# A decoder step's compressed branch: the prompt's chunks worked together with the first sample's, and one load of cache chunks moved forward

## The reference, cut to what matters

```python
def nsa_compress(kv, w_ck1, w_ck2, w_cv1, w_cv2, pe_k, pe_v):
    ...
    def mlp(x, pe, w1, w2):
        x = (x + pe[None, None, :, None, :]).transpose(0, 3, 1, 2, 4).reshape(B, NSA_KV_HEADS, n_cmp, CMP_BLK * HEAD_DIM)
        return jax.nn.silu(x @ w1) @ w2
    kc = mlp(blocks[:, :, :, 0], pe_k, w_ck1, w_ck2)
    vc = mlp(blocks[:, :, :, 1], pe_v, w_cv1, w_cv2)
```

## Time and profile before

| | us |
|---|---|
| median of 3 runs (range) | 1182.02 (1179.38 to 1186.98) |
| the profiled execution, its own time | 1191.54 |
| its span in the trace | 1189.7 |
| PE, DVE, ACT, POOL busy | 1084.4, 617.1, 392.6, 69.9 |
| the key stage in the trace, from the prompt's last projection column to the last sample's keys | 182.8 to 455.0 |

### The profile page before, as it was taken

The page is one execution under the profiler, slowest core; times in us unless marked ns, Lnnn a source line. Parts: engine busy times, 40 slices in busy tenths (PEclk is TensorE's granted clock), DMA queues, the critical chain, the costliest instruction groups (busy, mean ns, idle before and its releaser), DMA issues.

```text
span 1189.7 us, 23077 instructions
## 1 busy us (share of the span) xinstructions
PE 1084.4 (91%) x8348; PEld 953.0 (80%) x8348; DVE 617.1 (52%) x1042; ACT 392.6 (33%) x725; POOL 69.9 (6%) x83
## 2 busy tenths in 40 slices
PE   3996999998989998989999898999999999999993
PEld 2996999887878886555555557999999999999993
DVE  4431673586778787765444436445543335553332
ACT  4120212333333335556444435332231112221223
POOL 2000001221112100000000000110000000000002
PEclk9998997798999896988999978999999999999997
DMA  7529218799999963256666651323333333332321
GB/s 248 178 79 222 79 40 230 188 241 246 268 265 275 273 209 115 90 187 202 212 200 205 212 177 36 89 71 88 88 106 89 94 85 89 94 97 72 90 71 72
DMA packets 180131, 177.61 MB, mean 149 GB/s; under 512 B 13063, under 2 KB 140676, under 8 KB 177700
## 3 DMA queue, kind: packets, MB, share of 16 engines
q1 hardware_dynamic: 178610, 171.33, 50.7%
q10 hardware_dynamic: 1458, 5.43, 1.4%
HBM read 170.83 MB, written 10.06 MB: 152 GB/s over the span
## 4 chain that ended last, share of the span: by engine, by line
PE 64%; SPq 18%; issue 6%; DMA 4%; DVE 3%; ACT 3%; POOL 0%; POOLq 0%; DVEq 0%; ACTq 0%
PE bank L662 59%; SPq L576 4%; PE bank L666 4%; SPq L498 3%; SPq L540 2%; SPq L564 2%; SPq L543 2%; SPq L491 2%; DMA low_arena<-in_cache_nsa_slc_kv_dram 1%; DMA low_arena<-in_consts_dram 1%; DMA high_arena<-in_cache_sb_kv_dram 1%; DMA high_arena<-in_w_in_dram 1%; ACT low_arena L1550 1%; SPq L504 0%; SPq L582 0%
## 5 line engine op out<-in xcount | busy, mean ns | idle before, releaser
L662 PE MATMUL bank<-high_arena 128*128 128x254 f32 (+8 forms) x1864 | 239.6, 346 | 16.5 <-DMA high_arena<-in_cache_sb_kv_dram 6.6
L662 PEld LDWEIGHTS bank<-high_arena 128*128 128x128 f32 (+5 forms) x1864 | 185.2, 152 | 53.6 <-issue 10.1
L2114 DVE TENSOR_TENSOR w_low<-high_arena,w_high 128x1024 fp32r<-128x1024 f32 x72 | 90.1, 1252 | 84.1 <-ACT w_high L1487 74.2
L666 PE MATMUL bank<-low_arena 128*128 128x128 f32 (+3 forms) x658 | 108.0, 309 | 28.0 <-DMA page_ids<-in_page_table_dram 14.7
L666 PEld LDWEIGHTS bank<-low_arena 128*128 128x128 f32 (+3 forms) x658 | 87.4, 164 | 39.6 <-issue 27.2
L1487 ACT ACTIVATE w_high<-high_arena 128x1024 fp32r<-128x1024 f32 x72 | 76.3, 1060 | 114.8 <-PE bank L662 113.8
L662 PE MATMUL bank<-a_high,w_high 128*128 128x256 f32 (+1 forms) x512 | 104.3, 285 | 5.3 <-issue 2.9
L662 PE MATMUL bank<-h_high,w_high 128*128 128x256 f32 (+1 forms) x512 | 103.1, 283 | 1.8 <-DVE h_low L2141 1.8
L662 PE MATMUL bank<-a_low,w_high 128*128 128x256 f32 (+1 forms) x512 | 103.8, 284 | 0.0
L662 PE MATMUL bank<-a_high,w_low 128*128 128x256 f32 (+1 forms) x512 | 103.5, 283 | 0.0
L662 PE MATMUL bank<-h_low,w_high 128*128 128x256 f32 (+1 forms) x512 | 103.3, 283 | 0.0
(11 more groups left out here) (218 smaller groups left out, 1583.6 us busy)
## 6 DMA issues: line engine op xcount, KB each, us to landing
low_arena<-in_cache_sb_kv_dram SPq DMA_DIRECT2D x128, 256.0 KB, 4.9
high_arena<-in_cache_sb_kv_dram SPq DMA_DIRECT2D x128, 256.0 KB, 3.7
high_arena<-in_cache_nsa_cmp_kv_dram SPq DMA_DIRECT2D x128, 128.0 KB, 5.2
high_arena<-in_w_up_dram SPq DMA_DIRECT2D x32, 512.0 KB, 4.1
high_arena<-in_w_down_dram SPq DMA_DIRECT2D x32, 512.0 KB, 4.2
high_arena<-in_w_in_dram SPq DMA_DIRECT2D x10, 1136.0 KB, 5.6
low_arena<-in_cache_nsa_slc_kv_dram SPq DMA_DIRECT2D x128, 64.0 KB
high_arena<-in_cache_nsa_slc_kv_dram SPq DMA_DIRECT2D x128, 64.0 KB, 2.4
```

The source lines that it names most:

```text
L662: return T.matmul(out, lhsT=l, rhs=r, start=start, stop=stop, **k)
L666: return T.transpose(out, in_, ident[0:n, 0:n])
L2114: V.tensor_tensor(w_lo_r[u], w_raw[u], w_hi[u], ALU.subtract).then_inc(sem(f"w_lo{u}"), 1)
```

## The change

1. The prompt has no turn of its own. Its chunks are transposed first (`prompt_chunks_T`, 16 transposes), copied by ACT into `xTp`; in the turn of sample 0 each weight w1 is used three times in a row: for the prompt's 62 columns, for one column of `pe`, and for the sample's 254. All three results lie in the same PSUM bank. The 32 matmuls with one column that stood ahead of the prompt's turn are gone from there, and so are the waits of PE, ACT and DVE for `pebias`.
2. ACT does the sigmoid of sample 0 as six activations (prompt's and sample's), after a wait for `pebias`. DVE takes the bias out of PSUM (`bias(kv)`) after the quarter that ends each of the two sums, and so waits in the turn of sample 0 at four places: after pages 6, 8, 10 and 14.
3. The chunks of sample 1 (16 DMAs) are issued in the projection, behind the last w_in block, into a buffer moved to the end of memory; the prompt's chunks get a landing buffer of their own. `load_keys(0, 0)` loads no chunks.
4. SP waits for `snew` only ahead of the last ring buffer (page 7), not ahead of the stage.
5. POOL's waits are put in terms of transposes done in the same half. Loops start at 1, with turns 0 written out.

```diff
@@ -332,10 +333,14 @@
         w2 = [view(x_at + 4096 + i * DH, DH) for i in range(2)]
         pebias = view(x_at + 4224, 4)
         xT = [view(hT_at + i * 2048, KD, KVH, P) for i in range(2)]
-        nat_at[1] = r.take(4096)
+        nat_at[1] = TOTAL - 304 - 4096
+        nat_p = view(kc_at, CH // 2, 2, KVH, DH)
+        xTp = view(r_at, 2, KD, KVH, NCP + 1)
         nat = [[view(nat_at[u] + 2048 * half, CH // 2, 2, KVH, DH) for half in range(2)] for u in range(2)]
         hid = [view(r.take(256), KVH, P) for _ in range(4)]
         qb = view(r.take(2 * 512), 2, 512)
+        hidp = [view(r.take(KVH * NCP), KVH, NCP) for _ in range(4)]
+        assert r.at <= nat_at[1]
...
             load_columns(*COLUMNS[1])
+            for half in range(2):
+                load_chunks(page_ids(NPG + 8 * half), 1, half)
...
+                        if p == 7:
+                            sp.wait_ge(sem("snew"), 2)
...
-            sp.wait_ge(sem("snew"), 2)
-
-            with sp.Fori(0, 3) as i:
+
+            load_keys(0, 0, False)
+            load_keys(0, 1, True)
+            with sp.Fori(1, 3) as i:
...
-            for kv in range(2):
-                for m in range(16):
-                    ins = mm(bank[6][:, kv:kv + 1], w1[kv][:, m, :], vcol[:, 24 + 16 * kv + m:25 + 16 * kv + m],
-                             m == 0, m == 15)
-            ins.then_inc(sem("start_pe"), 1)
             for j in range(2):
                 pe.wait_ge(sem(f"qkT_ev{j}"), 7)
             pe.wait_ge(sem("qkT_ev0"), 8)
-            pe.wait_ge(*signal("pebias", 2))
...
+            def prompt_chunks_T(kv, qp):
+
+                pe.wait_ge(sem("perm"), kv + 1 + 1)
+                pe.wait_ge(sem(f"xT_ev{qp}"), kv + 1)
+                n = 2 * (NCP + 1)
+                for j in range(2):
+                    for hh in range(KVH):
+                        t = 2 * (2 * qp + j)
+                        ins = tr(bank[qp][:, (2 * j + hh) * P:(2 * j + hh) * P + n],
+                                 per(kv, hh, 0)[0:n, t:t + 2, :].rearrange("p t d -> p (t d)"))
+                ins.then_inc(sem(f"xT_mm{qp}"), 1)
...
+                    outp = bank[2 + kv][:, 256:256 + KVH * NCP].rearrange("p (h c) -> p h c", h=KVH)
                     for m in (2 * qp, 2 * qp + 1, 2 * qp + 4, 2 * qp + 5):
-                        mm(out, w1[kv][:, m, :], xT[kv][:, m, :, 0:nb], m == 0, False)
-                        ins = mm(out, w1[kv][:, 8 + m, :], xT[kv][:, m, :, 1:nb + 1], False, m == 7)
+                        for f in range(2):
+                            begin, end, w_ = m == 0 and f == 0, m == 7 and f == 1, w1[kv][:, 8 * f + m, :]
+                            if prompt:
+                                mm(outp, w_, xTp[:, kv, m, :, f:NCP + f], begin, end, skip_group_check=True)
+                                at = 24 + 16 * kv + 8 * f + m
+                                mm(bank[2 + kv][:, 320:321], w_, vcol[:, at:at + 1], False, end, skip_group_check=True)
+                            ins = mm(out, w_, xT[kv][:, m, :, f:NC + f], begin and not prompt, end, skip_group_check=prompt)
...
+            for kv in range(2):
+                for qp in range(2):
+                    prompt_chunks_T(kv, qp)
+            compress(0, key_work(0, 0), True)
+            compress(1, key_work(0, 1))
+            with pe.Fori(1, 4) as i:
                 for u in range(2):
-                    todo = [lambda: keys_T(i, u, 0)]
-                    for q in range(4):
-                        todo.append(lambda q=q: (key_scores(i, u, q), keys_T(i, u, q + 1)))
-                    todo.append(lambda: key_scores(i, u, 4))
-                    compress(i * 2 + u, 2, lambda: todo.pop(0)())
+                    compress(i * 2 + u, key_work(i, u))
...
-            act.wait_ge(*signal("pebias", 2))
...
+            def prompt_chunks_out(kv, qp):
+                act.wait_ge(sem(f"xT_mm{qp}"), kv + 1)
+                S.activation(xTp[:, kv].rearrange("p (f q) h c -> p f (q h) c", f=2)[:, :, 4 * qp:4 * qp + 4, :],
+                             bank[qp].rearrange("p (a c f) -> p f a c", a=4, f=2)[:, :, :, 0:NCP + 1],
+                             ACT.Copy).then_inc(sem(f"xT_ev{qp}"), 1)
+
+            def sample_keys(i, u, prompt=False):
...
+                    if prompt:
+                        act.wait_ge(*signal("pebias", kv + 1))
+                    both = [(hid[kv][:, :, 0:NC], 0, NC)] + ([(hidp[kv], 256, NCP)] if prompt else [])
+                    for e, at, n in both:
+                        ins = S.activation(e, bank[2 + kv][:, at:at + KVH * n].rearrange("p (h c) -> p h c", h=KVH),
+                                           ACT.Exp, bias=pebias[:, 2 + kv:3 + kv], scale=-1.0)
+                    chain(ins)
+                    for e, at, n in both:
+                        ins = S.activation(e, e, ACT.Ln, bias=K("one"))
+                    chain(ins)
+                    for e, at, n in both:
+                        ins = S.activation(e, e, ACT.Exp, scale=-1.0)
+                    ins.then_inc(sem(f"hid_e{kv}"), 1)
...
+            def bias(kv):
+
+                dve.wait_ge(sem(f"hid_mm{kv}"), 1)
+                col = bank[2 + kv][:, 320:321]
+                chain(V.tensor_copy(pebias[:, kv:kv + 1], col))
+                V.tensor_scalar(pebias[:, 2 + kv:3 + kv], col, -1.0, None, ALU.mult).then_inc(sem("start_dve"), 1)
+
+            def silu(c, kv, prompt=False):
+
+                dve.wait_ge(sem(f"hid_e{kv}"), c + 1)
+                dve.wait_ge(sem(f"w2_mm{kv}"), c + 1)
+                for at, n, hid_ in ((256, NCP, hidp), (0, NC, hid))[0 if prompt else 1:]:
+                    hp = bank[2 + kv][:, at:at + KVH * n].rearrange("p (h c) -> p h c", h=KVH)
+                    ins = V.scalar_tensor_tensor(out=hid_[2 + kv][:, :, 0:n], in0=hp, scalar=pebias[:, kv:kv + 1], in1=hid_[kv][:, :, 0:n],
+                                                 op0=ALU.add, op1=ALU.mult)
+                ins.then_inc(sem(f"hid_ready{kv}"), 1)
...
+            sb_keys(0, 0, 0, 6)
+            bias(0)
+            sb_keys(0, 0, 6, 8)
+            silu(0, 0, True)
+            sb_keys(0, 0, 8, 10)
+            bias(1)
+            sb_keys(0, 0, 10, 14)
+            silu(0, 1, True)
+            sb_keys(0, 0, 14, 16)
+            compressed_out(0, True)
+            sample_work(0, 1)
```

More of the change, by code:

```diff
@@ L194, with __init__ @@
 class Turns:
-    def __init__(self, chain, count, per):
-        self.chain, self.count, self.per = chain, count, per
+    def __init__(self, chain, count, per, start=0):
+        self.chain, self.count, self.per, self.start = chain, count, per, start
     def __enter__(self):
@@ L202, in __enter__ @@
         self.first = c.n
-        self.loop = c.eng.Fori(0, self.count)
+        c.n = self.base = c.n - self.start * self.per
+        self.loop = c.eng.Fori(self.start, self.start + self.count)
         i = self.loop.__enter__()
@@ L210, in __exit__ @@
         if e[0] is None:
-            assert c.n - self.first == self.per, (c.n - self.first, self.per)
+            assert c.n - self.base == self.per, (c.n - self.base, self.per)
         c.off = 0
@@ L772, in key_scores, with compress @@
                 ins.then_inc(sem("qs_mm"), 1)
[L774 to L778, removed]
+            def prompt_chunks_T(kv, qp):
[8 more added lines that the diff above has]
+                ins.then_inc(sem(f"xT_mm{qp}"), 1)
+            def compress(c, between, prompt=False):
                 def chunks_T(kv, s):
                     half, qp = s % 2, s // 2
[L782 to L785, removed]
+                    pe.wait_ge(sem("perm"), c * 4 + (2 * kv + half + 3) + 1)
+                    pe.wait_ge(sem(f"xT_ev{half}"), c * 4 + (kv * 2 + qp + 2) + 1)
                     for j in range(2):
@@ L833, in compress, with key_work @@
                 ins.then_inc(sem("w2_mm1"), 1)
-            compress(0, 1, lambda: None)
-            with pe.Fori(0, 4) as i:
-                for u in range(2):
-                    todo = [lambda: keys_T(i, u, 0)]
-                    for q in range(4):
-                        todo.append(lambda q=q: (key_scores(i, u, q), keys_T(i, u, q + 1)))
-                    todo.append(lambda: key_scores(i, u, 4))
-                    compress(i * 2 + u, 2, lambda: todo.pop(0)())
+            def key_work(i, u):
+                todo = [lambda: keys_T(i, u, 0)]
+                for q in range(4):
+                    todo.append(lambda q=q: (key_scores(i, u, q), keys_T(i, u, q + 1)))
+                todo.append(lambda: key_scores(i, u, 4))
+                return lambda: todo.pop(0)()
@@ L1310, in chunks_out @@
                                  ACT.Copy).then_inc(sem(f"xT_ev{half}"), 1)
                 def sigmoid(kv):
[L1313 to L1318, removed]
@@ L1319, in sigmoid @@
-                    S.activation(e, e, ACT.Exp, scale=-1.0).then_inc(sem(f"hid_e{kv}"), 1)
+                    act.wait_ge(sem(f"hid_mm{kv}"), c + 1)
```

(23 more changed lines are left out.)

146 lines of the change are left out of this document (67 added, 79 removed).

## The result

The changed kernel takes 1196.92 us (median of 4 runs, 1192.16 to 1202.32) against 1183.24 for the kernel before, timed beside it (4 runs): a ratio of 1.0117, with a 95% interval of 1.0062 to 1.0172. It is slower by some 13.7 us where I had forecast 1180 and a range up to 1193. The profiled execution took 1196.94, its span 1195.1: only 5.4 us more than the profiled execution of before (1191.54), which lay 9.5 above its kernel's median, so the two profiles can't be subtracted to give the loss.

The account below looks back on a forecast made before the run. The prediction took SP's DMA issues, 29.8 us a sample, to bound the middle of the key stage. An earlier start of 1.6 us, kept to the end, gave 1182.0 - 1.6 = 1180.4, say 1180; range 1171 to 1193 (8 in 10).

Parts of the forecast that it names:

- Quarters on PE: PE's turn of sample 0: each quarter takes 6.85 us against 3.43, the first starting at 203.2.
- load-paced value: PE's quarters in sample 0: the longer of stream and next weight load sets each step, 0.856 us a weight.
- the low clock: Slower rival: PE's clock stays at 0.50 in sample 0, quarters cost 13.7 us, total 1208; chance 0.12.
- loads that do not hide: Rival in sample 0: PE's weight loads are not overlapped, quarters take 9.4 us, total 1190.5; chance 0.06.
- DVE and the ring: Samples 0 and 1: DVE's bias waits delay pages, SP waits about 7 us for ring buffers; 1.9 of 10.7 us survive.
- The rival by which the ring doesn't hold SP: Faster rival in sample 1: page buffers are free in time, SP keeps its 10.7 us lead, total 1171; chance 0.16.
- Sample 1's turn: On PE, after the second silu and the w2 matmuls: starts near 246.5, 1.1 us earlier than 247.59.
- The third group of keys: In sample 1's turn on PE: its load lands at 260.0, PE arrives at 260.3, 1.6 us earlier than before.
- The loads in the projection cost nothing: In the projection: 16 issues need about 9 us and fit in SP's 21.7 us wait for the rotation.
- the stretch at SP's pace: Middle of the key stage, paced by SP's issues: starts 1.6 us earlier and keeps that to the stage's end.
- The sum: Whole kernel: -1.6 us, taken over from the profiled execution to the median, 1182.0 to 1180.4.

Follow-up runs that it names:

- N = 256: The changed kernel with 128 idle waiting instructions put on SP in the projection, ahead of its key loop: 1190.6 us, 1.0046 of the kernel before.
- DVE's new order: The changed kernel with DVE doing eight pages ahead of each bias wait in sample 0: 1189.79 us, 1.0032; with SP's loop also written out, 1182.21 us, 0.9975.

## Why the prediction was wrong

*Quarters on PE.* Forecast 0.856 us a weight at full clock, first quarter at 203.2; measured 0.88 and 203.26, and clock 0.99 and 1.00 in the two stretches above. The load-paced value held. The rivals of the low clock and of loads that do not hide are refuted. One reading in the low clock's paragraph was wrong: ahead of the rise at 313.2 PE did not only transpose. The granted clock fell at about 309.7, and PE ran matmuls, 16 records from 308.69, until its transposes began at 311.19. The rise at about 204.1 in the changed kernel has 24 transposes from 198.60 and then 0.9 us of matmuls ahead of it, so no row here shows the clock rising after transposes alone. (What the prediction cites from the Trainium skill on weight loads stands on its page under "The mechanism".)

*DVE and the ring.* DVE idle some 12 us ahead of `bias(1)`'s copy at about 239: 12.93 and 239.18. SP ready for sample 1 at 224.6: 224.18. Its eighth page issued by 249.4: 248.81. PE before the third quarter waits 1.4: 1.02. The rival by which the ring doesn't hold SP is refuted by 12.9 us of waits at `L552`. I had given 7 for sample 1's first half, and 6.4 of the 12.9 lie there; 6.1 lie in sample 0, ahead of pages 6 and 7.

*Sample 1's turn* at 246.5: it started at 247.38, 0.9 later, so that of the 1.1 us gained there only 0.2 were real. The third group of keys, forecast 1.6 us earlier, came at 261.64, 0.3 earlier than 261.94.

*The loads in the projection cost nothing:* right, the projection's wait fell from 21.7 to 13.0 and nothing behind it moved. Their worth was probably more than I gave them.

*The step that failed* is the sentence that the stretch at SP's pace "starts 1.6 us earlier, and keeps that to the end of the stage", with "nothing in the middle adds to it or takes from it" and "29 to 30 us from sample to sample after that". SP took 36.2 us for sample 3, and in this profile 32.9 for sample 2 and 32.8 for sample 6, where it doesn't stall. I had read SP's pace as a property of its issues, and looked at the two samples that the diff writes out ahead of the loop as the same instructions in another form. They moved the loop's body by 304 instructions in SP's code, and there its branch back stalls. The runs show this from both sides: 304 or 52 idle instructions give the unchanged kernel the loss, 97 take it away from the changed one, and writing the loop out takes it away too. A stall shows as 4 to 6 us and costs more than that: two cost the kernel before 1.21 and 1.34% (14 to 16 us, 7 to 8 each), and one costs the changed kernel 1.009 against 1.0027, 7 us on the same chip, though the run with N = 256 (128 instructions) shows less, 1.0046. I put the part beyond the stall itself down to the time behind it, in which the DMA engines are full again and can't catch up; this is argued, not shown. The window of the earlier trace rows in the changed kernel:

```profile
339.00:396.00 57.00, 45.29 (x266) 40.34 (x264) 39.92 (x63) 17.20 (x34) 8.93 (x14) 0.91 1.07 260
```

PE is busy 45.3 of 57 us where it was 51.9, at a DMA share of 1.07. Not all of that is the stall's: without one, this window has 53.3 in the changed kernel and 49.8 in the kernel before, each with its loop written out. How the deficit divides among the last samples was not measured.

*The sum.* Without the stall the change is worth 0.9986 (loop written out) or 1.0027 (loop moved) of the kernel before. My -1.6 us (0.9986) lies inside the first interval and just below the second, which starts at 0.9993; zero lies inside both. So the small gain is neither shown nor refuted. Against the kernel before with its own loop written out, 0.9965, the change gains nothing that can be told. None of the versions is faster than that one; written out with DVE's new order, 0.9975, is the best form of the changed kernel.

The Trainium skill (Runtime: NRT & Kernel Launch, "Instruction fetch mechanics") says that a taken branch to code that is no longer among the two pages held by the engine has to wait for a DMA fetch. The traces agree in kind, with 4.2 to 5.7 us at each such branch. They disagree on the size of a page: it says 16 KB, and the packets of SP's queue are of 8 KB (those of `q8` are of 16), and the pattern repeats with 128 instructions, since moving the loop by 128 or by 256 left it stalled. Two pages of 256 instructions would hold the body at 111 to 443, at 163 to 495 and at 543 to 879 alike, and only the first was free. This rule, with the place of the loop in each kernel's code, is the rival that the prediction lacked. The earlier trace rows could not show it: in the kernel before the branches cost 0.27 and 0.23.

## What to carry to other kernels

When a diff writes part of a loop out on an engine whose issues set the pace, count the instructions that it puts ahead of the rest of the loop and ask what the branch back costs at its new place; look in the chain of waits for a long `issue` on the loop's own line, and at the number of instruction packets. A comparison of two versions can be decided by code that neither meant to change: move the loop with idle instructions, or write it out in both, before you give the time to the edit. Here that was worth 0.5 to 1.3%, and the edit itself nothing measurable.

## What I had not expected of the hardware

- SP's branch back cost 0.23 to 0.27 us at two places in its code and 4.18 to 5.73 at five, for nearly the same loop body (333 and 337 instructions). The DMA share in the last whole microsecond ahead of the branch was 0.71 to 1.12 at the stalled ones and 0.75 to 1.12 at the others.
- 8 KB of SP's code came as one packet, and a stalled loop brought some five more of them for each branch back (33 against 28).
- In each of the nine stalls one such packet started 1.6 to 1.8 us before SP went on.
